# The last head's turns in a retention layer, moved between parts of output slabs

## The reference, cut to what matters

```python
def retention_mix(h, s0, pos, w_in, w_out, norm_g):
    proj = h @ w_in
    q, k, v, g = jnp.split(proj, SPLIT1, axis=-1)
    q = rope(q.reshape(bsz, length, RET_HEADS, RET_DK), pos)
    k = rope(k.reshape(bsz, length, RET_HEADS, RET_DK), pos) * (RET_DK ** -0.5)
    y, s_last = retention(q, k, v, s0)
    y = head_norm(y, norm_g).astype(h.dtype)
    return (jax.nn.silu(g) * y) @ w_out, s_last
```

## Time and profile of the kernel before

| | |
|---|---|
| median of 3 runs | 1935.55 us (1934.4 to 1935.87) |
| the profiled execution | 1934.12 us, of which the span of its instructions 1932.3 us |
| mean granted clock of TensorE | 0.972 |
| TensorE busy | 1837.8 us, 95% of the span |
| VectorE, ScalarE, GpSimd busy | 49%, 33%, 45% |
| slabs' matmuls (L316) | 3 groups of 4288, 899.8, 891.1 and 884.4 us |

### The profile page before, as it was taken

How to read it: one execution, slowest core, us unless ns; L and a number is a source line. 1 busy time by engine, 2 the same in 40 slices (tenths; PEclk the granted TensorE clock), 3 DMA queues, 4 the chain that set the end, 5 groups by cost and what they waited for, 6 DMA issues and landing times.

```text
span 1932.3 us, 34346 instructions
## 1 busy us (share of the span) xinstructions
PE 1837.8 (95%) x14081; PEld 1779.9 (92%) x14081; DVE 949.2 (49%) x1526; ACT 629.0 (33%) x913; POOL 861.5 (45%) x431
## 2 busy tenths in 40 slices
PE   5969989899999999999899999999799999999996
PEld 5969977799999999999899999999699999999996
DVE  4264765556652452455644443344455524525555
ACT  5333422234322222234433332233234422222342
POOL 3352332246554454456543333433155544544562
PEclk8989979899999999999999999999899999999998
DMA  5212211012233222223222222222112222232221
GB/s 211 77 44 69 77 44 44 23 55 88 88 110 132 88 87 99 85 68 109 77 80 75 79 79 76 85 79 75 52 65 77 88 97 88 87 99 82 66 95 46
DMA packets 49472, 156.76 MB, mean 81 GB/s; under 512 B 5984, under 2 KB 10208, under 8 KB 49376
## 3 DMA queue, kind: packets, MB, share of 16 engines
q1 hardware_dynamic: 43200, 145.57, 21.7%
q10 hardware_dynamic: 6176, 9.83, 1.5%
HBM read 149.75 MB, written 5.63 MB: 80 GB/s over the span
## 4 chain that ended last, share of the span: by engine, by line
PE 87%; DVE 8%; ACT 2%; issue 1%; DMA 1%; POOL 0%; SPq 0%; DVEq 0%; POOLq 0%; ACTq 0%
PE proj L316 78%; PE Q L926 7%; DVE arena L1659 1%; ACT arena L623 1%; DVE rstd L366 1%; DVE op_lo L386 1%; DMA w_raw<-in_w_v 1%; DVE arena L1510 0%; ACT op_hi L373 0%; DVE arena L1326 0%; PE Q L1159 0%; DVE v_tok L1416 0%; DVE x L1661 0%; PE proj L926 0%; DVE arena L1284 0%
## 5 line engine op out<-in xcount | busy, mean ns | idle before, releaser
L411 POOL TENSOR_TENSOR w_lo<-w_raw,w_hi 128x1024 fp32r<-128x1024 f32 (+2 forms) x276 | 651.6, 2361 | 785.4 <-ACT w_hi L337 785.0
L316 PE MATMUL proj<-op_hi,w_hi 128*128 128x256 f32 x4288 | 899.8, 291 | 28.6 <-DVE op_lo L386 18.6
L316 PE MATMUL proj<-op_hi,w_lo 128*128 128x256 f32 x4288 | 891.1, 289 | 0.0
L316 PE MATMUL proj<-op_lo,w_hi 128*128 128x256 f32 x4288 | 884.4, 288 | 0.0
L316 PEld LDWEIGHTS proj<-op_hi,w_hi 128*128 128x128 f32 x4288 | 690.4, 190 | 38.8 <-issue 16.3
L316 PEld LDWEIGHTS proj<-op_lo,w_hi 128*128 128x128 f32 x4288 | 693.2, 190 | 0.0
L316 PEld LDWEIGHTS proj<-op_hi,w_lo 128*128 128x128 f32 x4288 | 688.5, 189 | 0.0
L337 ACT ACTIVATE w_hi<-w_raw 128x1024 fp32r<-128x1024 f32 (+2 forms) x276 | 284.7, 1032 | 731.6 <-PE proj L316 727.6
L1326 DVE TENSOR_TENSOR arena<-proj,rstd 128x512 f32<-128x512 f32 x145 | 100.1, 691 | 232.6 <-PE proj L316 197.8
L1333 DVE TENSOR_TENSOR x<-proj,x 128x512 f32<-128x512 f32 x72 | 49.8, 692 | 261.6 <-PE proj L316 261.6
L926 PE MATMUL Q<-arena 128*128 128x256 f32 (+9 forms) x524 | 119.3, 378 | 11.4 <-DVE arena L1520 7.5
(11 more groups left out here) (159 smaller groups left out, 1017.3 us busy)
## 6 DMA issues: line engine op xcount, KB each, us to landing
w_raw<-in_w_gu SPq DMA_DIRECT2D x88, 512.0 KB, 3.2
w_raw<-in_w_down SPq DMA_DIRECT2D x32, 512.0 KB, 3.2
w_raw<-in_w_heads_a SPq DMA_DIRECT2D x30, 512.0 KB, 3.3
w_raw<-in_w_heads_b SPq DMA_DIRECT2D x18, 512.0 KB, 3.2
w_raw<-in_w_gate SPq DMA_DIRECT2D x16, 512.0 KB, 3.2
w_raw<-in_w_xbc SPq DMA_DIRECT2D x12, 512.0 KB, 3.2
w_raw<-in_w_down SPq DMA_DIRECT2D x16, 384.0 KB, 3.0
w_raw<-in_w_v SPq DMA_DIRECT2D x8, 512.0 KB, 8.0
```

The source lines that it names most:

```text
L316: last = nc.tensor.matmul(proj[:, 2 * g.mod(2) + half, 0:size], w[:, lo:lo + P], o[:, at:at + size], start=(k == 0 and j == 0), stop=(k == ...
L411: nc.gpsimd.tensor_tensor(w_lo[:, c:c + width], w_raw[:, c:c + width], w_hi[:, c:c + width], ALU.subtract).then_inc(w_lo_done, 1)
```

## The change

In the last head's last slab, TensorE now does turn1 of that same head, half of the slab (four eighths), turn2, and the other half. In `drain` turns 3, 4 and 5 remain. Between them stand parts of the first two slabs of ret_b: four eighths of slab 0 behind turn3; two more of slab 0 and four of slab 1 behind turn4; two more of slab 1 behind turn5. Then the last two eighths of slab 0, those of slab 1, and the remaining six slabs whole and written out one after the other, where a loop was. `slab` gets an argument `ks`, the eighths to do; the waits for weights and PSUM go with eighth 0, the signal that the slab is done with eighth 7. ScalarE and VectorE do their parts of turns 1 and 2 of the last head ahead of their work on its last slab. GpSimd's and SyncE's orders stay as they were.

```diff
-        def slab(pe, ph, n, ops, ready=None, k0=0):
+        def slab(pe, ph, n, ops, ready=None, k0=0, ks=None):
...
-            pe.wait_ge(w_lo_done, (s + 1).v)
+            ks = range(ph.kt) if ks is None else ks
+            if 0 in ks:
+                pe.wait_ge(w_lo_done, (s + 1).v)
             for m in range(ph.m):
                 g = (n * ph.m) + (ph.g0 + m)
-                if g.k or g.c >= 2:
+                if 0 in ks and (g.k or g.c >= 2):
                     pe.wait_ge(tile_read, (g + -1).v)
-                for k in range(ph.kt):
+                for k in ks:
...
-                last.then_inc(tile_done, 1)
+                if ph.kt - 1 in ks:
+                    last.then_inc(tile_done, 1)
...
@@ ScalarE: head and drain
+                        last = not h.k and h.c == RH - 1
                         for r_ in range(6):
+                            if last and r_ == 5:
+                                turn1(h)
+                                turn2(h)
...
                     def drain():
-                        turn1(At(7))
-                        turn2(At(7))
                         turn4(At(7))
                         turn5(At(7), At(6))
@@ TensorE: head and drain
+                        last = not h.k and h.c == RH - 1
                         for r_ in range(6):
                             if not first and r_ < 5:
                                 turns[r_](h + -1)
+                            if last and r_ == 5:
+                                turn1(h)
+                                slab(pe, PH[name], n + r_, 1, ks=range(0, 4))
+                                turn2(h)
+                                slab(pe, PH[name], n + r_, 1, ks=range(4, 8))
+                                continue
...
+                    ready_b = (sem("r_mlo"), 9)
+
+                    def early(n, ks):
+                        slab(pe, PH["ret_b"], At(n), 0, ready_b, ks=ks)
+
                     def drain():
-                        for turn in turns:
-                            turn(At(7))
+                        turn3(At(7))
+                        early(0, range(0, 4))
+                        turn4(At(7))
+                        early(0, range(4, 6))
+                        early(1, range(0, 4))
+                        turn5(At(7))
+                        early(1, range(4, 6))
                     heads(pe, head, lambda: phase("ret_a", 0, (sem("r_mlo"), 1)), drain)
-                    phase("ret_b", 0, (sem("r_mlo"), 9))
+                    for n in range(2):
+                        early(n, range(6, 8))
+                    for n in range(2, KD):
+                        early(n, None)
@@ VectorE: head and drain
+                last = not h.k and h.c == RH - 1
                 for r_ in range(6):
+                    if last and r_ == 5:
+                        turn1(h)
+                        turn2(h)
...
             def drain():
-                for turn in (turn1, turn2, turn3, turn4):
-                    turn(At(7))
+                turn3(At(7))
+                turn4(At(7))
                 turn5(At(7), At(6))
```

## The result

The changed kernel takes 1916.85 us (median of 4 runs, 1916.11 to 1917.84), the kernel before 1934.97 us beside it (4 runs, 1933.82 to 1935.87). The ratio is 0.9907 with a 95% interval of 0.989 to 0.9924. Predicted were 1917.0 us. The profiled execution took 1916.11 us with a span of 1914.3, 18.0 less than before.

A forecast was written before the change was run, and what follows sets the result against it. TensorE, busy 95% of the span, was taken to bound the kernel. Of 20.06 us to win, stalls of 1.35 leave 18.72; 1935.55 - 18.7 = 1916.85, said as 1917.0 us, range 1915 to 1923.

The forecast's parts named there:

- Turns 1 and 2: In the last head's last slab: both covered without a stall, turn2 by 0.14 us only, ending at 1368.93 and 1373.02.
- Turns 3 and 4: Behind the last slab: no stalls, since waits of 2.53 and 2.45 us are covered; ends at 1378.36 and 1385.69.
- Turn5: Last turn of the last head: needs normalised rows 5.22 us after turn4, so starts at 1390.91 after a 0.54 us stall.
- The low parts: Slab 0's last two eighths in ret_b need VectorE's low parts of the head: stalls of 0.77 and 0.04 us.
- The end of slab 1: ret_b's second slab ends at 1397.52 instead of 1416.24, a gain of 18.72 us.
- Cuts and loop: Slabs cut by turns cost 0 to 0.4 us more, taken as 0; writing out ret_b's loop on TensorE is worth 0.
- the change gives nothing: Rival: what follows ret_b doesn't follow TensorE, or early pieces wait for the last head; time 1935, chance 0.04.
- The second rival: Half clock from turn1 through ret_b's slab 1, turns lengthened by 1.86: time 1940, chance 0.03.
- Short waits and the clock: Waits of 1.11 us and less keep clock 1.00, 2.39 us loses it; the new order's longest stall is 0.77.
- The rule on transposes: If transposes don't count as busy, turn2 and turn5 lengthen the stalls around them, giving the first rival's sum.
- the first rival: The clock drops around turn5 if VectorE is late by a microsecond: 5.3 us together, time 1922, chance 0.11.
- one total of 20.06: The most to win between the last head's slabs and ret_b slab 1's end: waits, half-clock turns 3 to 5, slow first slabs.

The follow-up runs named there:

- the split held back: The changed kernel with GpSimd's split of ret_b slab 2's weights held until VectorE has done turn1 of the last head: 1917.8 us in one run.
- the kernel without waits: The changed kernel with the last slab split 4, 2, 2 eighths behind turns 1, 2, 3 and ret_b's pieces dealt out by wait lengths: 1915.61 us.
- the two kernels with less cover: The changed kernel with the six eighths of ret_b behind turn4 cut to two or to four, the rest behind turn5: 1920.47 and 1917.79 us.
- the parts alone: The changed kernel with turns 1 and 2 back behind the last slab, parts of ret_b still between turns 3, 4 and 5: 1926.51 us.
- the turns moved alone: The changed kernel with turns 1 and 2 in the last slab, but ret_b whole behind turn5: 1925.51 us.
- the discarded work: The changed kernel with the ten eighths of ret_b between turns 3, 4 and 5 thrown away and ret_b redone whole behind turn5: 1923.85 us.

## Why the prediction was right, point by point

- **Turns 1 and 2.** Laid out to 1368.93 and 1373.02, measured 1368.91 and 1373.13. Turn2's margin of 0.14 was just too small: VectorE's last operation for it, begun at 1371.43 and 0.33 long, ends at 1371.76, turn2's first transpose starts at 1371.82, and turn2 ends 0.11 late. The profile lists no wait for it; the kernel with the split held back shows it.
- **Turns 3 and 4.** Laid out to 1378.36 and 1385.69; the pieces behind them begin at 1378.47 and, behind turn4, 0.1 us later than laid out as well. Both ran at a head's prices. That a wait taken from the drain serves as the time a result needs in the new order was the step on which all covers rest, and it held.
- **Turn5.** A stall of 0.54 laid out, 0.57 measured, start at 1391.03 for 1390.91.
- **The low parts.** A stall of 0.77 laid out for the seventh eighth, 0.75 measured, at 1394.81 for 1394.48. Of the 0.33, 0.12 came with turn5's start. The rest is turn5 itself: from its start to the end of its last transpose it took 1.34 us (1391.03 to 1392.37), where I had taken the 1.11 of a head. Those count from the shown end of the matmul ahead, and the first transpose overlaps that matmul; behind a wait there is none to overlap. VectorE begins at 1392.40. The stall is the same because TensorE is as late as VectorE.
- **The end of slab 1.** Laid out at 1397.52. TensorE's next slab begins at 1398.00, and with the 0.2 us by which a read follows the last matmul that is 1398.2, 0.7 late. 0.33 of it stand above, 0.2 are that pipeline end, which I left off, and 0.15 are the pieces behind the stall. This is why 18.72 laid out became 18.03. That the median still came out 0.15 us from the forecast is luck: the kernel before took 1934.97 us beside it, 0.58 less than the 1935.55 from which the forecast counts, and this makes up for most of the 0.69. VectorE itself reads slab 1 only at 1400.82, since slab 0 and the work that follows it come first; by slab 3 (1410.18) it has caught up, and TensorE waits for none of it.
- **Cuts and loop.** Cuts were priced at 0 to 0.4 us and taken as 0. By the prices of the prediction, nine slabs (53.91) and the turns (11.00) with the pipeline end of 0.2 make a stretch of 65.11 us; the kernel without waits has 65.35. What is left for all its cuts is 0.24 us, within the bounds; its turn2 is held up as in the change, so the cuts by themselves cost less. The loop was 0, and measured 0.
- **The rivals.** The clock did not drop (1.00 through the stretch). Its mechanism was shown by the two kernels with less cover, behind waits of 3.56 and of 2.05 us, where I had gone by one of 2.39, and at a smaller price. That the change gives nothing, or runs at half clock throughout, was excluded by the span. The second rival's factor for half clock, 1.86, was read wrongly: it comes from turns 3 to 5 of the drain, and there the clock is back at 1.00 before turn4 ends (1394.55):

```profile
1392.80:1396.10 3.30, 1.74 (x7) 0.48 (x6) 1.53 (x5) 0.00 (x0) 0.00 (x0) 1.00 0.00 0
```

Turn3 alone gives 4.91 / 2.35 = 2.09. By that the turns at half clock are 21.8 us for 19.4, and that rival's time is 2.4 us longer.

- **Short waits and the clock.** The prediction read from the earlier trace rows that waits of 1.11 us and less leave the clock alone. That is true of the trace that it read. In the changed kernel's profiled execution the same two waits, in code that the change doesn't touch, lost it. TensorE and the clock in the changed kernel, then the clock before:

```profile
308.32 1.10 PE L1097 MATMUL Q<-ident,arena 128*128 128x128 f32 x8 [1.11 <-DVE arena L1578]
310.15 1.56 PE L1039 MATMUL Q<-ident,arena 128*128 128x128 f32 x8 [0.74 <-ACT arena L626]
311.00:313.00 2.00, 2.00 (x11) 2.00 (x10) 0.61 (x1) 1.10 (x2) 0.00 (x0) 0.50 0.00 0
```

```profile
311.00:313.00 2.00, 2.00 (x20) 2.00 (x19) 1.10 (x1) 1.47 (x3) 0.44 (x1) 1.00 0.00 0
```

In nine of the ten traces the clock stays at 1.00 at this place. That it held around turn5 with waits of 0.57 and 0.75 us is what all three traces with these waits show (the change, the parts alone, the split held back), and no rule.

- **The rule on transposes.** The Trainium skill, "TensorE: Matmul & The Clock Gate", Part 4, has it that a transpose doesn't count as TensorE being busy in the way that a matmul does. The runs here don't settle this. The price that the prediction put on it, the first rival's, did not come: the eight transposes of turn5 took 1.09 us in a stretch at 1.00. Behind waits of 2.05 and 3.56 us the clock fell after them; but behind 2.46 us it fell in turn4, which has none. In layer 0, TensorE has for 4.1 us (307.14 to 311.24 before) nothing but 18 transposes and the two waits above, and the clock holds in nine traces and falls in one.

What the prediction leaves open is the sum by parts. It gave one total of 20.06 and didn't divide it. Of the 18.03 that were measured, the discarded work gives 11.69 to the clock and the first waits and 6.34 to work done under the later ones.

## What to carry to other kernels

Where a chain of dependent steps on two engines has no work of its own left, look for a product that is summed in pieces behind it: the pieces whose inputs are ready can stand between the steps, in program order, and each wait measured in the old order says how many pieces it takes. Spread the pieces so that no wait stays at all where you can (here a kernel with TensorE busy for 65.33 of 65.35 us): a wait that leaves the clock alone in one trace can lose it in the next. Read a lost clock from the clock rows from the wait on, since the work behind the step that waited can be what pays. To tell the clock from the work, do the pieces once and throw them away.

## What the runs showed of the hardware

- **The clock can fall late.** Behind a wait of 3.56 us turn5's eight large transposes ran at full rate in 1.09 us, and turn5 ended at 1393.39; the clock was 0.87 from 1393 to 1394, and at 0.50 in the two microseconds that follow. Behind 2.05 us it was 0.92, then 0.50. So the step that waited isn't always the one that pays. It can be: the wait of 2.39 us in the earlier trace rows ended at 355.12, and the mean clock was 0.54 from 355 to 356 already; with the turns moved alone, turn4 ran its last 4.5 us at 0.64 behind 2.46 us.
- **The same waits can lose the clock in one execution and not in another.** Layer 0's 1.11 and 0.74 us, with transposes between, left it at 1.00 in nine traces, and in the changed kernel's it was at 0.50 behind them.
- **A fall costs 1.2 us here** (1.15 and 1.17), with slabs behind it that keep TensorE busy. Behind the drain of before, and around turn3 in the kernel with the parts alone, it lasted longer. In the latter TensorE, from the start of turn3, was busy for 8 us, 1381.90 to 1390.00, and all of them at 0.50.
- **One VectorE operation took nearly four times as long beside GpSimd.** A 128x512 product of two operands in SBUF took 2.58 us beside GpSimd's 2.40 us split, and 0.68 alone. The rows show it as waiting, not as sharing: the split ran from 1368.36 to 1370.76 and VectorE's operation ended 0.54 us behind it, at 1371.30; the split took 2.41 us without VectorE beside it. The Trainium skill, "SBUF — State Buffer", in its section "SBUF: two separate sides", says that VectorE with two inputs in SBUF and a GpSimd instruction that reads SBUF exclude each other for a whole instruction, the later one being held up; the trace agrees, 2.58 for 0.68.
